# Two VectorE gate operations of the gate-and-up chunks issued behind the next chunk's first seven-product group

## The reference, cut to what matters

```python
gate, up = _split(rms_norm(x, norm_ffn[i]) @ w_gate_up[i], (D_FF, D_FF))
x = x + (jax.nn.silu(gate) * up) @ w_down[i]
```

## Time and profile before

| | us |
|---|---|
| median of 3 runs | 2177.11 (2175.9 to 2177.83) |
| the profiled execution | 2178.24 |
| its span, first to last instruction | 2176.4 |
| TensorE busy | 2158.2 (99%) |
| TensorE weight loads busy | 1784.3 (82%) |
| VectorE busy | 1555.4 (71%) |
| ScalarE busy | 1095.3 (50%) |

### The profile page before, as it was taken

The page is one execution under the profiler, slowest core; times in us unless marked ns, Lnnn a source line. Parts: engine busy times, 40 slices in busy tenths (PEclk is TensorE's granted clock), DMA queues, the critical chain, the costliest instruction groups (busy, mean ns, idle before and its releaser), DMA issues.

```text
span 2176.4 us, 29853 instructions
## 1 busy us (share of the span) xinstructions
PE 2158.2 (99%) x10052; PEld 1784.3 (82%) x10052; DVE 1555.4 (71%) x1937; ACT 1095.3 (50%) x1414; POOL 58.4 (3%) x99
## 2 busy tenths in 40 slices
PE   8999999999999999999999999999999999999999
PEld 6888888888888888888888888888878888888887
DVE  6657766888888885555566767677888888874443
ACT  7755654545555554444444444454454545544332
POOL 2101100000000000000100000000000000000000
PEclk9999999999999999999999999999999999999999
DMA  8765466667666666666555656566676666666664
GB/s 313 233 194 155 138 211 204 202 194 222 202 206 214 214 217 199 205 205 202 177 172 164 202 158 191 172 206 209 195 221 203 205 208 217 201 219 218 202 203 133
DMA packets 244569, 435.57 MB, mean 200 GB/s; under 512 B 23040, under 2 KB 43648, under 8 KB 244480
## 3 DMA queue, kind: packets, MB, share of 16 engines
q1 hardware_dynamic: 243392, 432.31, 63.7%
q10 hardware_dynamic: 1088, 2.10, 0.2%
HBM read 411.25 MB, written 2.10 MB: 190 GB/s over the span
## 4 chain that ended last, share of the span: by engine, by line
PE 70%; DVE 11%; issue 7%; SPq 6%; DMA 4%; ACT 2%; DVEq 1%; ACTq 0%
PE unit_bank L1801 52%; SPq L408 5%; PE mix_bank L1853 4%; PE mix_bank L1801 4%; DMA raw<-in_w_gate_up 4%; PE unit_bank L1853 3%; DVE w_lo L1074 3%; PE unit_bank L1813 1%; PE mix_bank L1813 1%; PE mix_bank L1871 1%; DVE sums L1096 1%; ACT w_hi L615 1%; PE mix_bank L2001 1%; DVE up_ff L1574 1%; DVE act_ff L1598 1%
## 5 line engine op out<-in xcount | busy, mean ns | idle before, releaser
L1074 DVE TENSOR_TENSOR w_lo<-raw,w_hi 128x1024 fp32r<-128x1024 f32 x687 | 828.8, 1220 | 472.8 <-ACT w_hi L615 450.7
L615 ACT ACTIVATE w_hi<-raw 128x1024 fp32r<-128x1024 f32 x687 | 719.0, 1057 | 603.4 <-PE unit_bank L1801 381.9
L1801 PE MATMUL unit_bank<-w_hi,gT_hi 128*128 128x512 f32 x704 | 217.1, 389 | 1.3 <-issue 1.3
L1801 PE MATMUL unit_bank<-w_lo,gT_hi 128*128 128x512 f32 x704 | 216.9, 389 | 0.0
L1801 PE MATMUL unit_bank<-w_hi,gT_lo 128*128 128x512 f32 x704 | 216.8, 389 | 0.0
L1801 PE MATMUL unit_bank<-w_hi,hT_hi 128*128 128x512 f32 (+1 forms) x576 | 181.2, 396 | 0.0
L1801 PE MATMUL unit_bank<-w_hi,hT_lo 128*128 128x512 f32 (+1 forms) x576 | 176.2, 387 | 0.0
L1801 PE MATMUL unit_bank<-w_lo,hT_hi 128*128 128x512 f32 (+1 forms) x576 | 175.9, 387 | 0.0
L1801 PEld LDWEIGHTS unit_bank<-w_hi,gT_hi 128*128 128x128 f32 x704 | 132.0, 188 | 29.4 <-issue 2.0
L1801 PEld LDWEIGHTS unit_bank<-w_lo,gT_hi 128*128 128x128 f32 x704 | 132.2, 188 | 27.5
L1801 PEld LDWEIGHTS unit_bank<-w_hi,gT_lo 128*128 128x128 f32 x704 | 132.2, 188 | 27.4
(11 more groups left out here) (348 smaller groups left out, 3113.9 us busy)
## 6 DMA issues: line engine op xcount, KB each, us to landing
raw<-in_w_gate_up SPq DMA_DIRECT2D x352, 512.0 KB, 4.2
raw<-in_w_down SPq DMA_DIRECT2D x176, 512.0 KB, 4.6
raw<-in_w_in_b SPq DMA_DIRECT2D x104, 512.0 KB, 4.0
raw<-in_w_o SPq DMA_DIRECT2D x64, 512.0 KB, 4.4
raw<-in_w_in_a SPq DMA_DIRECT2D x40, 512.0 KB, 3.9
moved<-turned SPq DMA_DIRECT2D x528, 32.0 KB, 2.6
raw<-in_w_mem_kv SPq DMA_DIRECT2D x31, 512.0 KB, 5.6
tanh_ff<-act_ff SPq DMA_DIRECT2D x112, 32.0 KB, 3.3
```

What stands on the lines that cost most here:

```text
L615: act.activation(w_hi[:, s, :, :], raw[:, s, :, :], ACT.Copy).then_inc(sems["hi_ready"], 1)
L1074: dve.tensor_tensor(w_lo[:, s, :, :], raw[:, s, :, :], w_hi[:, s, :, :].bitcast(F32), ALU.subtract).then_inc(sems["lo_ready"], 1)
L1801: ins = pe.matmul(all_banks[2 * pair + tile][:, 0:cols], stationary[part][:, kt + j, tile * P:(tile + 1) * P], b[:, s, j, 0:cols], start=o ...
```

## The change

VectorE's `gate_silu` of the loop's chunks moves from step 1 to step 3. Nothing else changes: the plain `gate_silu` of the down projection stays at step 1, and TensorE, ScalarE, GpSimd and SyncE have the same instructions in the same order.

```diff
                 def chunk(j, own, shared):
 
                     for i in chunk_pieces():
-                        if i == 1:
+                        if i == 3:
                             gate_silu()
                         if i == 5:
                             times_up()
```

## The result

| | before | after |
|---|---|---|
| median, us | 2177.47 (2175.9 to 2178.12, 4 runs) | 2198.55 (2197.46 to 2198.6, 4 runs) |
| the profiled execution, us | 2178.24 | 2198.51 |
| its span, us | 2176.4 | 2196.6 |
| TensorE / weight loads / VectorE busy, us | 2158.2 / 1784.3 / 1555.4 | 2167.5 / 1781.8 / 1556.8 |

The changed kernel is slower: 1.0097 of the time before, 95% interval 1.0079 to 1.0114, or 21.1 us. VectorE does the same work. TensorE's granted clock is 1.00 in both. TensorE's "busy" grows by 9 us though its matmuls are the same, because a matmul is recorded with 0.39 us where the next one would start after 0.23, so that the first part of each wait counts as busy.

A forecast was written before the change was run, and what follows sets the result against it. A loop of VectorE, SyncE, DMA and ScalarE, closing once a chunk, bounds the kernel. 1.20 us added less 0.12 gained is 1.08 a chunk, 20 times +21.6 us on 2178.24, carried to the median: 2198.7 us, range 2189 to 2204.

The forecast's parts named there:

- The loop bounds the chunks: Waits through VectorE, SyncE, DMA and ScalarE close once a chunk in 42.46 us; 1.08 us put in lengthens it; chance 0.62.
- 0.12 us gained ahead of the group: Without gate operations ahead, the first seven group starts 0.12 us sooner a chunk, then held by ScalarE's L634.
- 0.68 us at piece 6: Piece 6's low part comes 1.08 us later against 0.56 us of room, so TensorE stands 0.68 us later.
- 1.20 us uncovered behind it: Behind the first group nothing hides the two gate operations: 1.20 us ahead of piece 6's low part, 1.08 us remaining.
- rival "nothing": VectorE's 1.74 us wait ahead of the second group makes good the 1.20 us moved: 2177 us, chance 0.07.
- The sum: 1.08 us a chunk, 20 times: +21.6 us on the profiled execution's 2178.24 us, 2198.7 us at the median.
- the second group is released by TensorE itself and moves with TensorE: At the second seven group, ScalarE's 3.49 us and VectorE's 1.74 us waits depend on TensorE, so the group moves with it.
- 0.79 us of lateness foreseen there: At piece 14, w_lo would end 1.08 us later, at 538.65, putting TensorE 0.79 us behind.
- the waits for `sums_lo`: Sign in the new profile: TensorE's waits for the seven groups' result, 13.9 us before, fall a little, not to nothing.
- those for a plain `w_lo`: Sign: TensorE's waits for plain pieces' low parts rise from 10 to 30 or 40, with 10 to 20 us in all.
- The sign against the loop: If piece 6 waits and SyncE's moves start no later against TensorE, the loop is wrong and only piece 6 costs.
- The rival "only piece 6": Moves and loads have hidden slack, so only TensorE's piece 6 wait costs, 0.68 us a chunk: 2190.7 us, chance 0.18.

The follow-up runs named there:

- spread_before: Kernel before with SyncE's 16 moves issued 4, 4, 4, 4 behind the loads of pieces 11 to 14 instead of 6, 6, 4: 2167.20 us, ratio 0.9957.
- gates_at_5: Kernel before with the gate operations at step 5, behind pieces 6 and 7 and right ahead of times_up: 2201.82 us, ratio 1.0110.
- half: Kernel before with only the second token tile's gate operation moved to step 3, the first's left at step 1: 2187.2 us, ratio 1.0048.
- thin_after: Changed kernel with SyncE's moves issued 4, 3, 3, 3, 3 behind the loads of pieces 11 to 15: 2188.58 us, ratio to the kernel before 1.0053.
- the thinner spread: Kernel before with SyncE's moves issued 4, 3, 3, 3, 3 behind the loads of pieces 11 to 15: 2166.78 us, ratio 0.9954.

## Why the prediction was right

2198.7 us was forecast and 2198.55 measured. Point by point:

- **The loop bounds the chunks.** Shown from both sides: shortening it by fewer moves ahead of loads 12 to 14 gives 0.49 us back and turns the chain over to TensorE (spread_before), and 1.20 us put in gives 1.06 (after: 43.85 - 42.79) and still does with piece 6 and the second group on time (gates_at_5). That 0.60 us put in gives 0.47 (half) fits.
- **0.12 us gained ahead of the group.** L1094 starts 0.03 us behind L634 in the chunk above (509.30 + 1.49 = 510.79, then 510.82), and without the gate operations the kernel before gains 2.1 us, 0.10 us a chunk (0.06 by the distance of first groups).
- **0.68 us at piece 6.** TensorE is 0.69 us later there in the chunk above, and 0.67 in the mean of the 20 chunks.
- **1.20 us uncovered behind it.** The rows show 1.21. The idle 1.74 us ahead of the second group, the rival "nothing", does not help, since piece 6 and the transposes stand in between. The Trainium skill ("Perfetto Trace Analysis", section Identifying the Most-Contended Engine) takes the engine with the highest occupancy for the most-contended one and says to optimize it first. The page does not say that work on the other engines is free; read in that way, as the rival had it, it would have put the move at nothing, and 1.2 us a chunk on VectorE, busy for 71%, cost 21.1 us.
- **The sum.** 1.08 a chunk against 1.06 measured. 20 times that is 21.2 us, and the profiled execution is 20.3 us longer.
- **A step that failed: "the second group is released by TensorE itself and moves with TensorE".** In 15 of 20 chunks it waits for the load of piece 11, which `w_lo` of piece 7 releases, right behind the load of piece 10. I had followed the moved work to piece 6 and to the transposes, not to the loads behind these two pieces. The room was there to read: before, load 11 lands 13.82 us behind the start of the first group in the mean, and L634 of the second starts at 14.15 (522.51 - 508.36), only 0.33 us later. It did not change the sum, because the loop was the longer of the two: TensorE paid at the second group part of what it would have paid at piece 14 (0.79 us of lateness foreseen there), as gates_at_5 shows, where it pays at pieces 13 and 14 (14.6 and 8.3 us in all). Of the signs that I named, one missed by this step: the waits for `sums_lo` were to fall a little and rose by 4.5 us. Another missed in size: those for a plain `w_lo`, 37 times as forecast, are 23.7 us and not 10 to 20 (piece 6 alone 18.7). The sign against the loop did not show: the first move starts 523.74 - 519.97 = 3.77 us behind TensorE's piece 6, 520.07 - 516.81 = 3.26 before, so the moves do start later against TensorE.
- **The rival "only piece 6" at 0.68 us a chunk** is no correct reading of what is left without the loop, for it lacked the second group. thin_after stands 12.6 us above the kernel before, close to its 13.6, but over its own base it is 1.10 us a chunk, of which piece 6 has some 0.7 and the second group the rest. The closeness to 13.6 is chance.

That 1.08 us a chunk came out so near is partly luck too: two paths, the loop and TensorE by way of piece 6 and the second group, end within half a us of each other (43.85 and 43.43 us).

## What to carry to other kernels

A TensorE that is 99% busy can still be paced by others: follow the chain of waits over one turn of the loop, and if it closes without a TensorE line, what is put into it lengthens every turn, however idle its engine is on average. It does not follow that what is taken out of it is gained: the chain of the earlier trace rows ran through the gate operations where they stood (4.4%), and leaving them out gave 0.1 us of 1.2 a chunk, for a second path, the load of piece 5 and ScalarE's rounding, ended right behind. Of a step that is moved, follow everything that it now stands ahead of, and the loads that those instructions release as well. Before moving work around such a loop, look for its longest link and shorten that: here it was 16 small DMA issues in one queue ahead of a load. Dealing them out more thinly, a change of one line, gave 9.5 us (2167.20 us; 2166.78 with the thinner spread).

## What had not been expected

How much time SyncE's issues take: six moves take 3.69 us, and with 16 of them and two loads the way to load 14 is 11.4 us of issuing alone (520.07 to 531.48 in the kernel before, 523.74 to 535.14 in the kernel after), in a chunk of 42.8 us. Two rows of the kernel after, six moves and the load behind them:

```profile
523.74 3.69 SPq L408 DMA_DIRECT2D moved<-turned  x6
527.69 0.37 SPq L393 DMA_DIRECT2D raw<-in_w_gate_up  x1
```
